# Attention scores of two heads issued behind each other on TensorE, and the turning of q and k taken apart from their norm

## The reference, cut to what matters

```
aq = _rmsnorm(heads(aq, 8), qk_gain_q); ak = _rmsnorm(heads(ak, 8), qk_gain_k)
attn = _neighbourhood_attention(aq, ak, heads(av, 8), rpb) * silu(az)
# in it, for one grid row r:
s = einsum('bhwd,bhiwjd->bhwij', q_r, k_sel) * Dh ** -0.5 + bias
p = softmax(s)                      # over the 8 x 16 keys
o = einsum('bhwij,bhiwjd->bhwd', p, v_sel)
```

## Time and profile before

| | us |
|---|---|
| median of 3 runs | 2290.59 (2287.72 to 2292.43) |
| the profiled execution | 2285.26 |
| its span, first to last instruction | 2283.5 |
| PE busy | 2183.6 (96%) |
| DVE, ACT, POOL busy | 1094.7, 946.2, 389.5 |
| granted TensorE clock, mean | 0.977 |

### The profile page before, as it was taken

One profiled execution on the slowest core, in us unless ns is written; L12 is line 12 of the kernel. 1 busy time (PEld: TensorE's weight loads), 2 busy tenths in 40 slices (PEclk: granted clock), 3 DMA queues, 4 the chain that ended last, 5 costly groups with the idle time before them and its releaser, 6 DMA issues.

```text
span 2283.5 us, 29031 instructions
## 1 busy us (share of the span) xinstructions
PE 2183.6 (96%) x11559; PEld 1786.2 (78%) x11559; DVE 1094.7 (48%) x2025; ACT 946.2 (41%) x1713; POOL 389.5 (17%) x594
## 2 busy tenths in 40 slices
PE   8899899999796999999999999999999999999998
PEld 5678677777696888888887888877888888888886
DVE  5676535442157343566555655645514342433441
ACT  4655445444365143556455644643213223232220
POOL 5010632832103120000000000004301121010011
PEclk9999999999798999999999999999999999999999
DMA  4355445331833331121111111112211112344332
GB/s 142 120 178 195 125 112 156 76 78 33 324 120 92 135 117 47 37 60 52 46 47 33 60 47 47 37 47 70 71 59 56 45 49 73 107 153 143 97 102 88
DMA packets 169672, 209.76 MB, mean 92 GB/s; under 512 B 36320, under 2 KB 122816, under 8 KB 168000
## 3 DMA queue, kind: packets, MB, share of 16 engines
q1 hardware_dynamic: 148848, 140.71, 19.9%
q0 software_dynamic: 20688, 67.19, 9.4%
HBM read 150.41 MB, written 53.77 MB: 89 GB/s over the span
## 4 chain that ended last, share of the span: by engine, by line
PE 86%; DVE 5%; ACT 3%; DMA 2%; issue 2%; POOL 1%; SPq 1%; DVEq 0%; ACTq 0%; POOLq 0%
PE PS L1762 13%; PE PS L1764 13%; PE PS L1763 13%; PE PS L1756 9%; PE PS L1758 9%; PE PS L1757 9%; PE PS L1722 5%; PE PS L2047 3%; PE PS L2026 3%; PE PS L1856 2%; PE PS L1833 2%; DVE WH L2476 1%; PE PS L2079 1%; PE PS L2092 1%; DMA WHF<-xe_d 1%
## 5 line engine op out<-in xcount | busy, mean ns | idle before, releaser
L1762 PE MATMUL PS<-WH,HH 128*128 128x512 f32 x1344 | 548.0, 408 | 4.2 <-DVE WH L2476 2.2
L1764 PE MATMUL PS<-WH,HL 128*128 128x512 f32 x1344 | 528.0, 393 | 0.0
L1763 PE MATMUL PS<-WH,HH 128*128 128x512 f32 x1344 | 527.2, 392 | 0.0
L1756 PE MATMUL PS<-HH,WH 128*128 128x512 f32 (+1 forms) x976 | 401.2, 411 | 21.0 <-DVE WH L2476 21.0
L1758 PE MATMUL PS<-HH,WH 128*128 128x512 f32 (+1 forms) x976 | 384.0, 393 | 0.0
L1757 PE MATMUL PS<-HL,WH 128*128 128x512 f32 (+1 forms) x976 | 383.6, 393 | 0.0
L1762 PEld LDWEIGHTS PS<-WH,HH 128*128 128x128 f32 x1344 | 254.8, 190 | 61.9 <-issue 9.3
L1764 PEld LDWEIGHTS PS<-WH,HL 128*128 128x128 f32 x1344 | 254.1, 189 | 55.3
L1763 PEld LDWEIGHTS PS<-WH,HH 128*128 128x128 f32 x1344 | 255.0, 190 | 45.4
L2476 DVE SCALAR_TENSOR_TENSOR WH<-RAW,WK,WH 128x512 fp32r<-128x512 f32 (+2 forms) x248 | 186.4, 775 | 202.0 <-ACT WH L2101 201.6
L1756 PEld LDWEIGHTS PS<-HH,WH 128*128 128x128 f32 (+1 forms) x976 | 183.9, 188 | 60.3 <-DVE WH L2476 22.6
(11 more groups left out here) (317 smaller groups left out, 2902.1 us busy)
## 6 DMA issues: line engine op xcount, KB each, us to landing
RAW<-in_w_in SPq DMA_DIRECT2D x200, 256.0 KB, 2.9
RAW<-in_w_out SPq DMA_DIRECT2D x32, 256.0 KB, 3.6
sig_d<-WK POOLq DMA_DIRECT2D x32, 256.0 KB, 2.4
WK<-sig_d POOLq DMA_DIRECT2D x32, 256.0 KB, 3.1
WK<-in_rpb POOLq DMA_DIRECT2D x16, 480.0 KB, 4.7
RAW<-in_w_in SPq DMA_DIRECT2D x32, 192.0 KB, 3.0
dnc_d<-TM SPq DMA_DIRECT2D x12, 512.0 KB, 3.9
TM<-dnc_d SPq DMA_DIRECT2D x10, 512.0 KB, 4.8
```

The costliest lines, as they stand in the source:

```text
L1756: e.matmul(ps, wh, hh, start=k == 0, stop=False)
L1762: e.matmul(ps, hh, wt[:, 0:width], start=k == 0, stop=False)
L1763: e.matmul(ps, hh, wt[:, 512:512 + width], start=False, stop=False)
L1764: mm = e.matmul(ps, hl, wt[:, 0:width], start=False, stop=k == 7)
```

## The change

1. `na_front` becomes one stream for both heads: scores of query tile i of head 0 and head 1 are put directly behind each other, once `np` of both heads two tiles back is known. The engine code takes head 1's wait ahead of head 0's matmul, so that nothing stands between the two.
2. `work()` charges head 1's scores 60 ns on PE.
3. The turning `nt` gets a stream of its own, `na_turn(p)`. It waits for the norm `nm` and for the last scores of both heads of the pair ahead, no longer for `nw`; `nq` and `nm` run on without it.
4. Both bias tables of a half are asked for behind the scores of head 1.

```diff
@@ work()
-        return {"ns": [("pe", 2.2 * n), dve(n + 90), act(n + 340)], "np": [("pe", 340), act(384)],
+        return {"ns": [("pe", 60 if a[1] else 2.2 * n), dve(n + 90), act(n + 340)], "np": [("pe", 340), act(384)],
@@ na_side
             put("nm", p, u)
             yield
+
+    def na_turn(p):
+        for u in range(4):
+            yield has("nm", p, u)
             if p:
-                yield has("nw", p - 1)
+                yield has("ns", p - 1, 0, 7)
+                yield has("ns", p - 1, 1, 7)
             yield lambda: "na" in claims
             turn("nt", p, u)
             yield
@@ na_front
-    def na_front(p, h):
+    def na_front(p):
         for i in range(8):
             if i % 4 == 0:
                 yield has("nt", p, 2 + i // 4)
             if i > 1:
-                yield has("np", p, h, i - 2)
-            put("ns", p, h, i)
+                yield has("np", p, 0, i - 2)
+                yield has("np", p, 1, i - 2)
+            plan.both(("ns", p, 0, i), ("ns", p, 1, i))
             if i % 4 == 3:
+                table()
                 table()
             yield
@@ rows, and the blocks' loop
+        plan.spawn(na_front(p))
         for h in range(2):
-            plan.spawn(na_front(p, h))
             plan.spawn(na_back(p, h))
...
             plan.spawn(na_side(int(name[2])))
+            plan.spawn(na_turn(int(name[2])))
@@ TensorE, kind "ns"
-                    if i > 1 or p:
-                        w.wait_ge(*at["ns", p if i > 1 else p - 1, h, (i - 2) % 8, "s"])
+                    for head in (0, 1) if h == 0 else (1,):
+                        if i > 1 or p:
+                            w.wait_ge(*at["ns", p if i > 1 else p - 1, head, (i - 2) % 8, "s"])
```

## The result

The changed kernel takes 2283.3 us, the median of 7 runs (2281.4 to 2289.8), against 2290.6 for the kernel before, timed beside it. The ratio, worked out from all runs of both (that of the two medians is 0.9968), is 0.9975, 95% interval 0.9964 to 0.9986. It is 7.3 us faster, less than half of the 18 us forecast. Both lie above the kernel before's, 2285.3, which is a quick one of its kind. So a stage can be compared in the traces, but the 7.3 us of the medians can't be added up from them.

The account below looks back on a forecast made before the run. TensorE (PE) was taken to bound the attention stage, busy 320.4 of 335 us. The terms, -19.5 - 3.0 + 1 + 2 + 2 = -17.5 us, were rounded to a gain of 18, giving 2272.5 us; range 2262 to 2284.

Parts of the forecast that it names:

- term 4: Earlier turnings in the attention stage: projection steps fill PE either way, charged 0; bounds 3 us loss, about 10 gain.
- terms 1 to 3: PE's attention work: both heads' scores together -19.5 us, fewer entries into scores -3.0, more runs of projection steps +1.
- term 5: POOL's queue, pair 0: two table loads ahead of the fourth gather make PE stand 2 us; bounds 0 and 5.
- term 6: Block dz: ACT's first eviction waits about 4 us for the image's DMAs, PE stands 2; bounds 0 and 9.
- waits eat half: Rival: waits at pair 0's gather, dz's image and the turnings leave some -9 us, 2281; chance 0.15.
- The clock rival: More PE stretches at 1.2 GHz: 35 us more cancel the gain, 50 more end at 2298; chance 0.05.
- My own sign for being wrong: Attention stage: the forecast is wrong if PE's idle time there rises by over 10 us.
- The rule on evacuation: Rival: tiling doesn't speed up PSUM evacuation, which sets a pair's pace; sum near 0, 2290; chance 0.07.

Follow-up runs that it names:

- change_again: The changed kernel run once more, unchanged, beside three later kernels on the same chip; 2284.3 us, ratio 0.9960 to the kernel before.
- pair_only: The change with scores in pairs, but a pair's turnings waiting again for the writes of the pair ahead; 2276.9 us, ratio 0.9935 to the kernel before.
- turn_only: The kernel before, scores by head as they were, with only the change's early turnings; 2293.3 us, ratio 1.0006 to the kernel before.
- early_tables_slack: The change with early turnings, pair 0's table loads moved, and 0.9 us more slack between scores and transposes; 2265.5 us, ratio 0.9896 to the kernel before.
- early_tables: The change with early turnings kept and only pair 0's table loads moved later; 2294.7 us, ratio 1.0007 to the kernel before.

## Why the prediction was wrong

**What failed is the sentence of term 4, "projection steps fill PE either way", and with it the assumption under the sum, that 22 us less work leave PE's waits as they were but for 4 us.** The work did go: 309.9 to 288.2 us at full clock (`change_again`), 21.7 us where terms 1 to 3 have 21.5. Waiting took back 14.3 us (28.8 - 14.5) and the lower clock 2.3 ((30.7 - 5.7 - 20.5) / 2). 21.7 - 14.3 - 2.3 is the 5.1 us by which the stage is shorter. By what ended them, the waits for ACT rose by 9.9 us (15.4 against 5.5) and those for a gather by 6.6, and those for DVE fell by 2.4.

1. *Scores together, fewer entries, more runs* (terms 1 to 3, -21.5): right. Slots of 0.68 and 0.86 for both heads, and every kernel with pairs has 286.3 to 288.7 us of work (but for the one whose pieces moved behind dz, 283.4), every one without 308.2 to 312.7.
2. *The turnings* (term 4, 0, bounds +3 to -10): wrong for the change. Waits for ACT rose from 5.5 to 15.6 us. Some are the turnings' own, 2.78 + 5 x 0.93; the largest, 3.5 us, also stands in `pair_only`. With joined pairs, early turnings cost 6 us in one comparison (across chips), 10 in a second and nothing in a third, so they are not dear in themselves. That they are dear where ACT's queue is late already is my reading; no run tests it alone.
3. *POOL's queue in pair 0* (term 5, +2, bounds 0 to 5): mis-sized, 5.1 and 6.6 us in the two profiles. I gave the loads their issue time of 0.6 us each. What held the gather is their 3.31 us wait for DVE, and a landing 1.8 us longer. `turn_only` has the same two loads ahead of the gather, and PE waits for it 0.6 us, so this order of the queue isn't dear by itself. Moved alone, the loads gave nothing back.
4. *The image and dz* (term 6, +2): 0 at dz, by about 1 us: I had the DMAs land 2.5 us too late and ACT come 3 us too early. At the first image, for which I had no term, ACT's copy was late instead: for the substitution in the change, where PE stood 2.78 us, and for `at_d` in two experiments, 8.6 and 8.9.
5. *The rest of the program*: I expected no change from dz's end on. From there to the end it takes 1706.6 us (2285.5 - 249.4 - 329.5, `change_again`) against 1702.6, with 70.1 instead of 65.9 us at the lower clock, which explains 2 of the 4. In the profile shown first it is 1709.7, with 86.7. The stretch before the stage was 3.1 us longer too (249.4 against 246.3). It varied from 245.4 to 249.4 over these kernels, and I have no cause for it.

Of the rivals, "waits eat half" came out in size, 2281 foreseen and 2283 measured. Its figure has a slip in it: the middle between -4.5 and -17.5 is -11, not -9, which gives 2279.6. And it came through ACT's copies and the gather, most of it in pairs 0 and 1, not through the place I gave it. The clock rival did not come: in the stage the lower clock took 2 to 3 us. My own sign for being wrong, idle time up by over 10 us, was met. The rule on evacuation that I weighed (the Trainium skill, "TensorEngine Tiling (Array Packing)", section Performance Considerations) does not hold as a bound here: ACT is busy 152 of 330 us. Yet with the heads joined its queue is late in places, and PE stood for it.

That the forecast's size was there to be had is shown: three orders with pairs, 0.9 us of slack and gathers free of table loads gave 2265.3 to 2266.5, 25 us under the kernel before and 18 under the change. In `early_tables_slack` the stage is 30.4 us shorter than before: 21.5 us of work, 1.5 of waiting and 7.4 of clock, which I had given no gain. What stays open is what in these orders does it (table 15's share is not tested alone), why 0.6 us of slack was not enough in the one order tried, and which share each wait has, since every edit reshuffles the whole order: single comparisons of two orders differ by waits that neither edit meant.

## What to carry to other kernels

When work is taken off the engine that bounds a stage, look at how early its inputs come, not only at how busy the others are: an engine at 45% can still be late at every hand-over, and the saved time turns into waiting until the order keeps more distance between producer and consumer. In an in-order queue put what somebody waits for (here a gather) ahead of what waits itself (a table load that needs its buffer free), and count the wait of the one in front, not its issue time. And when one edit does nothing, try it together with the next suspect: slack alone and moved tables alone gained nothing on this change, both together 18 us. Then look whether the second edit did what it was meant to: here a stretch without projection steps went away with it, which neither edit was about.

## What the runs showed of the hardware

A wait on TensorE can cost more than itself. `early_tables` and `early_tables_slack` differ by the slack alone: idle 33.1 against 13.0 us, and the lower clock 41.0 against 6.8. Of these, 10.3 and 1.3 us are idle time anyway, so 20.1 us of waiting came with ((41.0 - 10.3) - (6.8 - 1.3)) / 2 = 12.6 us of lost clock; together they are the 32.3 us between the two stages, within 0.4. I had priced the clock as a rival of its own, apart from waits; here the two went together.

The lower clock also comes where PE hardly waits. None of the 20.5 us in the kernel before's stage falls in idle time; one stretch there, behind dense small pieces and a wait of 0.47 us, has PE busy throughout:

```profile
439.20:446.10 6.90, 6.90 (x22) 5.59 (x22) 2.44 (x7) 3.20 (x7) 6.20 (x11) 0.51 0.31 77
```

`turn_only` has 0.9 us more of idle time than the kernel before and 13.6 us more at the lower clock.

The landing time of a gather went with what stood ahead of it in the queue. Pair 0's fourth gather landed 5.1 to 5.6 us after its issue in the five kernels with two loads of 480 KB right ahead of it, and 2.1 to 3.8 us in the eleven with another gather there. And a change of one number in a planner moved the median by 29 us (2294.7 to 2265.5, 25 us by the ratios, since the two were timed on different chips) with the same instructions, more than the change under study.
